# Block kernel on one core: low halves of the weights moved between GpSimd and VectorE, a fifth K tile of the modulation on TensorE, and the sines moved into the values' round

## What is computed

```python
mod = silu(c) @ w_ada + b_ada                    # 1 x 3072
shift, scale, gate = split(mod, 3)
h = rms_norm(x) * (1 + scale) + shift            # 512 x 1024
q, k, v, z_attn, xbc, dt_raw, z_ssm = split(h @ w_in)
# 16 heads of 64, for query t and key s < t:
A[t, s] = sigmoid(z_ts) * prod_{s<j<t} (1 - sigmoid(z_tj))
xbc = silu(causal_depthwise_conv(xbc, conv_w, conv_b))
```

## Time and profile before

| | us |
|---|---|
| median of 3 runs | 1807.56 (1805.79 to 1808.59) |
| the profiled execution | 1804.74 |
| its span, first to last instruction | 1803.0 |
| PE busy | 1762.1 (98%) |
| DVE, ACT, POOL busy | 907.9, 761.4, 647.8 |
| mean granted clock of PE | 0.996 of full |

### The profile page before, as it was taken

One profiled execution on the slowest core, in us unless ns is written; L12 is line 12 of the kernel. 1 busy time (PEld: TensorE's weight loads), 2 busy tenths in 40 slices (PEclk: granted clock), 3 DMA queues, 4 the chain that ended last, 5 costly groups with the idle time before them and its releaser, 6 DMA issues.

```text
span 1803.0 us, 21919 instructions
## 1 busy us (share of the span) xinstructions
PE 1762.1 (98%) x8557; PEld 1413.6 (78%) x8557; DVE 907.9 (50%) x1332; ACT 761.4 (42%) x1243; POOL 647.8 (36%) x257
## 2 busy tenths in 40 slices
PE   7999999999999999999999999999999999999998
PEld 5787777768787867867988888888866898888886
DVE  7510588874977358953543333336457253333334
ACT  3323665556345353254532222226676442223222
POOL 1343222233235233433444444444410354444442
PEclk9999999999999999999999999999999999999999
DMA  8524322221122322311232223321310222322222
GB/s 307 196 94 117 90 63 59 72 71 47 66 101 78 127 71 70 105 48 59 81 107 93 93 94 101 107 95 62 101 56 1 94 94 97 107 99 93 93 93 82
DMA packets 83921, 166.05 MB, mean 92 GB/s; under 512 B 6041, under 2 KB 8222, under 8 KB 83838
## 3 DMA queue, kind: packets, MB, share of 16 engines
q1 hardware_dynamic: 83838, 164.93, 27.9%
HBM read 157.64 MB, written 2.10 MB: 89 GB/s over the span
## 4 chain that ended last, share of the span: by engine, by line
PE 75%; issue 16%; POOL 4%; DVE 3%; ACT 1%; DMA 1%; SPq 1%; POOLq 0%; DVEq 0%; ACTq 0%
PE PDT L689 12%; PE PDT L691 12%; PE PDT L690 12%; PE PDT L700 8%; PE PDT L701 8%; PE PDT L702 8%; POOL wlo L2006 4%; PE PM L1304 2%; PE PDT L1265 2%; PE PM L1265 1%; PE PM L1231 1%; PE PDT L830 1%; PE PDT L835 1%; PE PDT L829 1%; PE PM L1163 1%
## 5 line engine op out<-in xcount | busy, mean ns | idle before, releaser
L2006 POOL TENSOR_TENSOR wlo<-wraw,whi 128x2048 fp32r<-128x2048 f32 (+5 forms) x172 | 604.9, 3527 | 1011.3 <-ACT whi L1466 1011.3
L1466 ACT ACTIVATE whi<-wraw 128x2048 fp32r<-128x2048 f32 (+2 forms) x131 | 244.0, 1862 | 518.4 <-PE PDT L691 302.1
L700 PE MATMUL PDT<-hhi,whi 128*128 128x512 f32 x796 | 312.4, 392 | 1.9 <-POOL wlo L2006 1.9
L702 PE MATMUL PDT<-hhi,wlo 128*128 128x512 f32 x796 | 310.1, 390 | 0.0
L701 PE MATMUL PDT<-hlo,whi 128*128 128x512 f32 x796 | 310.1, 390 | 0.0
L689 PE MATMUL PDT<-whi,hhi 128*128 128x512 f32 (+1 forms) x592 | 234.0, 395 | 0.4 <-POOL wlo L2006 0.4
L691 PE MATMUL PDT<-whi,hlo 128*128 128x512 f32 (+1 forms) x592 | 227.9, 385 | 0.0
L690 PE MATMUL PDT<-wlo,hhi 128*128 128x512 f32 (+1 forms) x592 | 227.8, 385 | 0.0
L689 PE MATMUL PDT<-whi,mh_hi 128*128 128x512 f32 x512 | 199.3, 389 | 0.0
L690 PE MATMUL PDT<-wlo,mh_hi 128*128 128x512 f32 x512 | 199.2, 389 | 0.0
L691 PE MATMUL PDT<-whi,mh_lo 128*128 128x512 f32 x512 | 199.2, 389 | 0.0
(11 more groups left out here) (374 smaller groups left out, 2438.2 us busy)
## 6 DMA issues: line engine op xcount, KB each, us to landing
wraw<-in_mlp_w SPq DMA_DIRECT2D x64, 1024.0 KB, 5.2
wraw<-in_w_in SPq DMA_DIRECT2D x26, 1024.0 KB, 5.2
wraw<-in_even_w_in SPq DMA_DIRECT2D x16, 1024.0 KB, 5.3
w_ada<-in_w_ada SPq DMA_DIRECT2D x11, 1024.0 KB, 13.0
wraw<-in_w_out SPq DMA_DIRECT2D x8, 1024.0 KB, 5.2
swapped<-qk_sb SPq DMA_DIRECT2D x16, 256.0 KB, 7.4
wraw<-in_even_w_out SPq DMA_DIRECT2D x4, 1024.0 KB, 4.9
wraw<-in_odd_w_o SPq DMA_DIRECT2D x4, 1024.0 KB, 5.8
```

The costliest lines, as they stand in the source:

```text
L700: mm(bank, sth, hi[:, k0 + k, :], start=start and k == 0, stop=False)
L702: last = mm(bank, stl, hi[:, k0 + k, :], start=False, stop=stop and k == 3)
L1466: nc.scalar.activation(whi[base % 2][:, 0:n], wraw[base % 2][:, 0:n], ACT.Copy).then_inc(S("w_hi"), 1)
L2006: part = g.tensor_tensor(wlo[base % 2][:, cols], wraw[base % 2][:, cols], fl(whi[base % 2][:, cols]), ALU.subtract)
```

## The change

- **Entry.** PE takes a fifth K tile of the last scale chunk (`weigh(6, 3, 1)`), and DVE takes three instead of four. PE's two folds for the second half stand in the middle of the 16 low products of `first_half(0)`, not behind them. The low half of unit 1 is made by DVE after the second modulation; POOL's first is that of unit 2, and it waits for `w_split` 2. ACT copies the last half tile of the turned x, which DVE did.
- **Values' round.** ACT's sines stand in the second round of v, with the table change behind them. PE's first scores no longer wait for the eviction of v; the first values do.
- **Heads.** POOL makes the low halves of units 16 to 21 only after the convolution with the number in a list. The low half of unit 23 is made by DVE in head 13 (`dt_head`), before its squares; that of unit 24 by POOL after the eleventh convolution, that of unit 25 after the last `sb_split`. The low half of unit 22 is now 128 columns wide on POOL, where the loop made 2048.

```diff
-        def weigh(n, bank):
+        def weigh(n, bank, more=0):
...
-                last = mm(PM[:, bank, :], silu_w[:, 4 * (n % 2) + k, :], w[:, k, :], start=k == 0, stop=k == 3)
+                last = mm(PM[:, bank, :], silu_w[:, 4 * (n % 2) + k, :], w[:, k, :], start=k == 0,
+                          stop=k == 3 and not more)
+            for k in range(more):
+                pe.wait_ge(S(f"ada_loaded{n + 1}"), 16)
+                last = mm(PM[:, bank, :], silu_w[:, 4 * ((n + 1) % 2) + k, :], wview(ADA_SLOTS[n + 1], 4, 512)[:, k, :],
+                          start=False, stop=k == more - 1)
...
-                weigh(6, 3)
+                weigh(6, 3, 1)
             unit_wait(h)
             for f in range(4):
+                if h == 0 and f == 2:
+                    fold(2, 4)
+                    fold(3, 5)
...
-                fold(2, 4)
-                fold(3, 5)
...
             if pair:
                 pe.wait_ge(S("sb_out"), pair)
+            else:
+                phase_done(pe, "v")
...
-        for name in ("q", "k", "v"):
+        for name in ("q", "k"):
             phase_done(pe, name)
...
-        rounds("v", 2, lambda i, b: vo[:, b, bass.ds(i * 512, 512)])
+        u0 = PH["v"][0]
+        for r in range(2):
+            hi(0, u0 + 2 * r + 1, 0)
+            if r:
+                act.wait_ge(S("angles"), 1)
+                nc.scalar.activation(sinall[:, :, :], ang[:, :, :], ACT.Sin).then_inc(S("sines"), 1)
+                nc.scalar.activation(ang_s[:, :, :], ang[:, :, :], ACT.Sin, scale=0.5).then_inc(S("sines"), 1)
+                nc.scalar.preload_act_table_set("natural_log_exp_and_others")
+            hi(0, u0 + 2 * r + 2, 0)
+            for b in range(4):
+                full_wait(act, "v", b, r, u0 + 2 * r + 1)
+                nc.scalar.activation(vo[:, b, 512 * r:512 * r + 512], PD[b], ACT.Copy).then_inc(S(f"bank_free{b}"), 1)
...
-        pool.wait_ge(S("w_split"), 1)
-        pairs("q", 2)
+        pool.wait_ge(S("w_split"), 2)
+        for u in range(2, 5):
+            lo(0, u, 0)
...
-        pairs("xbc", 3)
-        pairs("z_ssm", 2)
-        lo(0, PH["dt"][0] + 1, 0)
-        pairs("z_attn", 2)
+        u0 = PH["xbc"][0]
+        for n, convolved in enumerate((0, 0, 0, 2, 3, 4, 6, 7, 8, 0)):
+            if convolved:
+                pool.wait_ge(S("conv_sum"), convolved)
+            lo(0, u0 + n + 1, 0)
+        u0 = PH["z_attn"][0]
+        pool.wait_ge(S("w_split"), u0 + 1)
+        pool.wait_ge(S("conv_sum"), XBC_T - 1)
+        lo(0, u0 + 1, 0)
+        pool.wait_ge(S("sb_split"), 3 * H1)
+        lo(0, u0 + 2, 0)
+        lo(0, u0 + 3, 0)
+        lo(0, u0 + 4, 0)
...
-        weigh(7, True, (3, 3))
+        weigh(7, True, (3, 3), 1)
         modulation(1)
+        dve.wait_ge(S("w_hi"), 2)
+        v.tensor_tensor(wlo[1][:, :], wraw[1][:, :], fl(whi[1][:, :]), ALU.subtract).then_inc(S("w_split"), 1)
...
+            if h == dt_head:
+                u = PH["z_attn"][0]
+                dve.wait_ge(S("w_hi"), u + 1)
+                dve.wait_ge(S("w_split"), u)
+                v.tensor_tensor(wlo[u % 2][:, :], wraw[u % 2][:, :], fl(whi[u % 2][:, :]), ALU.subtract)\
+                    .then_inc(S("w_split"), 1)
```

More of the change, by code:

```diff
@@ L1648, in _ @@
         turned_x(TT - 1)
+        act.wait_ge(S("xt_turned"), 2 * TT)
+        nc.scalar.activation(xt[:, 4:8, (TT - 1) * P:TT * P],
+                             PD[2 * ((TT - 1) % 2) + 1].rearrange("p (k c) -> p k c", k=4), ACT.Copy)\
+            .then_inc(S("xt_read1"), 1)
         def modulated(half):
@@ L1710, in after_piece @@
                 nc.scalar.activation(dst, PD[b], ACT.Copy, scale=scale).then_inc(S(f"bank_free{b}"), 1)
-        act.wait_ge(S("angles"), 1)
-        nc.scalar.activation(sinall[:, :, :], ang[:, :, :], ACT.Sin).then_inc(S("sines"), 1)
-        nc.scalar.activation(ang_s[:, :, :], ang[:, :, :], ACT.Sin, scale=0.5).then_inc(S("sines"), 1)
         hi(0, PH["xbc"][0] + 1, 0)
-        nc.scalar.preload_act_table_set("natural_log_exp_and_others")
         for h in range(H1):
@@ L2184, in turned_x, with weigh @@
                 .then_inc(S("xt_read1"), 1)
-        def weigh(n, fresh, row=None):
+        def weigh(n, fresh, row=None, k0=0):
             dve.wait_ge(S("ada_part" if n == 3 else f"ada_loaded{n if n < 8 else n - 4}"), 16 if n < 8 else 32)
             w, a = wview(ADA_SLOTS[n if n < 8 else n - 4], 4, 512), acc[n // 2][:, :]
-            for k in range(4):
+            for k in range(k0, 4):
                 col = silu_c[:, 4 * (n % 2) + k:4 * (n % 2) + k + 1]
@@ L2193, in weigh @@
                     dve.wait_ge(S("ada_loaded3"), 16)
-                if fresh and k == 0:
+                if fresh and k == k0:
                     op = v.tensor_scalar(a, w[:, k, :], col, None, ALU.mult)
@@ L2230, in _ @@
                 turned_x(t - 1)
-        turned_x(TT - 1)
         dve.wait_ge(S("c_ready"), 1)
```

## The result

| | before | after |
|---|---|---|
| median of the runs, us | 1806.67 (1804.32 to 1808.59, 4 runs) | 1791.65 (1791.57 to 1791.81, 4 runs) |
| profiled execution, us | 1804.74 | 1791.7 |
| its span, us | 1803.0 | 1790.0 |
| mean granted clock over the span | 0.996 | 0.997 |

The ratio is 0.9918, with an interval from 0.9906 to 0.9930. The kernel gained 13.0 us between the two profiled spans, where the prediction's sum was 13.1, and 15.0 us between the medians. Of these 2.85, 0.9 is that the kernel before has 1806.67 here and had 1807.56 when the forecast was made.

The account below looks back on a forecast made before the run. The prediction took PE, busy 98% of the span, as the bound. Its terms, 5.7 (entry) + 1.7 (head 0) + 5.7 (later heads) = 13.1 us, took the median from 1807.56 to 1794.5 us, range 1791.5 to 1799.

Parts of the forecast that it names:

- The bound: Whole kernel: PE is busy 98% of the span, so time falls only by what PE stands still or runs slowly.
- The entry, 5.7: Up to unit 4: shorter DVE multiplications, folds without the long wait and full clock gain 5.7 us.
- The forecast chain: Entry: unit 1 starts at 45.0 instead of 48.75, unit 1's low products end at 55.9, unit 4 lands by 71.7.
- the margins: Entry: slack of 1.0, 0.3 and 0; the rival that one or two waits stay gave 1797.5, chance 0.14.
- the 0.3 feared at unit 2: Entry: POOL's low half of unit 2 ready at 56.2, 0.3 after PE wants it.
- two of the signs: Entry, signs of being wrong: PE waiting for `wlo` at units 1, 2 or 4; ACT waiting for unit 4's load past 71.7.
- The clock behind the folds: Entry rival: folds count as rest, unit 1 begins at clock 0.50, 2.3 us not gained, 1796.8; chance 0.10.
- Head 0, 1.7: Head 0: moving the sines brings the tails to 182.35 instead of 184.05, a gain of 1.7 us.
- The sum did not get in beside POOL: Head 0 rival: DVE's two-tile sum runs beside POOL, 1.3 us more gain, 1793.2; chance 0.07.
- Heads, 5.7: Heads 4 to 15: waits of heads 7, 11 and 15 (3.8) and head 13 (1.86) vanish, together 5.7 us.
- Theory B: Posed after the result: much of the gain, and the 2 us beyond the sum, is clock no longer falling behind PE's waits.
- Theory C: Posed after the result: parts of the change do nothing, so a few lines bring the whole gain.

Follow-up runs that it names:

- pool_unit1: Changed kernel with unit 1's low half back on POOL, fifth K tile kept: 1795.45 us, ratio 0.9939.
- the second trace: Profile of the changed kernel run once more, nothing altered: 1791.61 us, ratio 0.9911.
- four_tiles: Changed kernel with four K tiles on each side, no fifth on PE: 1791.19 us, ratio 0.9915.
- both_four_tiles: Changed kernel with unit 13's low half held until head 0's `sb_split`, unit 4's load ahead of the gate's weights, and no fifth K tile: 1789.83 us, ratio 0.9905.
- late13: Changed kernel with POOL's low half of unit 13 held until head 0's `sb_split` is complete: 1788.57 us, ratio 0.9896.
- the first experiments: Earliest follow-up runs, with the kernel before run beside them; the text does not list which ones are meant.
- entry_only: Only the entry of the change, values' round and heads as in the kernel before: 1801.82 us, ratio 0.9966.
- no_conv_wait: Changed kernel without POOL's waits for the convolutions: 1794.19 us, ratio 0.9926.
- rest_only: Only the values' round and heads of the change, entry as in the kernel before: 1797.07 us, ratio 0.9945.
- pool_unit23: Changed kernel with unit 23's low half back on POOL: 1794.65 us, ratio 0.9932.
- xt_back: Changed kernel with the copy of the last x tile back on DVE: 1790.54 us, ratio 0.9913.

## Why the prediction was right, point by point

**The bound.** Right. PE is busy 98% before and after, and the time fell by what PE stood or ran slowly.

**The entry, 5.7.** Right in its chain (pool_unit1), and right in its size when counted from unit 0. From unit 0's first product to unit 4's it is 84.11 - 26.15 = 57.96 before, 79.91 - 27.47 = 52.44 after, and 78.62 - 26.18 = 52.44 in the second trace: 5.5. The ends of these stretches before are:

```profile
26.15 1.88 PE L963 MATMUL PDT<-hhi,whi 128*128 128x512 f32 x4 [1.77 <-ACT hhi L1654]
...
84.11 0.50 PE L700 MATMUL PDT<-hhi,whi 128*128 128x512 f32 x1
```

By the clock times of the first trace only 4.2 is left, since 1.3 went at 14 to 17.5 us. The forecast chain, moved by these 1.3, holds: unit 2 at 57.2 (measured 57.13), ACT's start on unit 4 at 73.0 (72.85). Of the margins only that of unit 4 was used up. PE waited 0.55 for it, where the step had 0.1: POOL's low half took 4.93, not 4.8, and PE was there a little earlier (79.36 against 78.3 + 1.3). The 0.3 feared at unit 2 did not come: POOL is through at 57.01, and the first product that uses the low half starts at 57.62. So two of the signs that the prediction had named for being wrong came: a wait of PE for `wlo` at unit 4, and ACT's start on unit 4 past 71.7. The first is 0.55 instead of the 0.1 in the sum, and the second is the late start of 1.3; neither touches the chain.

**The clock behind the folds.** The rival fails here: with no wait, 16 folds leave the clock at 1.00. With a wait of 0.53 (four_tiles) or 0.55 (both_four_tiles) among them it fell, one trace of each; with 0.45 (late13) it stayed.

**Head 0, 1.7.** Right: from unit 4's first product to the tails 184.05 - 84.11 = 99.94 before and 98.11 after, so 1.83. The sum did not get in beside POOL: it ended at 176.44, 0.28 after POOL (176.16), the very distance of the row that the step was built on. This is as the Trainium skill has it (SBUF — State Buffer, "SBUF: two separate sides"): the engine that comes second waits for the whole of the first one's instruction. The trace agrees to within 0.14, as the sum takes 0.42 alone and ended 0.28 after POOL. late13 shows it from the other side: with POOL later the sum takes 0.43, and another 1.68 is there.

**Heads, 5.7.** The waits went as said, in heads 7, 11, 13 and 15, and nothing was late behind `conv_sum`. The term was too small. From the tails of head 0 to those of head 15 it is 398.13 - 184.05 = 214.08 before and 385.19 - 178.02 = 207.17 after: 6.9. The tails of head 15 before, with the wait that is gone:

```profile
398.13 0.45 PE L1034 MATMUL PM<-sb_hi,neg_ge 128*128 128x384 f32 x1 [1.08 <-DVE sb_lo L2353]
```

Around the single waits the traces give 1.77, 1.77, 2.15 and 1.23 for 1.37, 1.36, 1.86 and 1.08. So a wait cost about 0.15 to 0.4 more than its idle time, which the sum did not count. A part of it can be read from the traces. A product lasts 0.39, but the next one starts 0.23 behind its start; a wait is counted from the end of the last product, which leaves 0.16 out. And the first one behind a wait is followed later than usual (in head 7 by 0.28 instead of 0.18), which is another 0.1. The rest stays open.

The terms of the trace, 4.2 + 1.8 + 6.9 = 12.9, are the 13.0 of the spans: the entry's shortfall of 1.5 and the heads' surplus of 1.2 nearly cancel. That 13.0 stands so close to 13.1 is therefore in part luck. Without the 1.3 at 14 to 17.5 us the terms are 5.5 + 1.8 + 6.9 = 14.2, and the term of the sum that was too small is the heads', 5.7 for 6.9.

**From the span to the median, 0 in the prediction, 2 in fact.** This is the step that was missing. The prediction left the distance from the profiled execution to the median as it was; it is 1.9 before (1806.67 against 1804.74) and none after (1791.65 against 1791.7). In before's 9 executions beside the first experiments the mean clock is 0.994 to 0.997 and the time 1804.52 to 1809.05, the fastest with 0.997. A mean clock that is 0.003 lower over 1803 us costs 5.4 us (an estimate: PE is busy nearly all the time), enough for all of this scatter. The profiled execution of before (0.996, 1804.74) was one of the better ones. The changed kernel has 0.997 to 0.998 and 1790.15 to 1791.87. So two waits of before had a second price, a fall of the clock behind them in some executions: 1.57 behind head 0's, 1.55 behind that of unit 23. Behind the waits of 1.36 in heads 7 and 11 no fall is in the traces that have them (before, entry_only, no_conv_wait). Theory B thus holds beside A for the scatter, and is the likely cause of the 2 us. That before's slower executions lose their time at these waits is argued from entry_only, rest_only and pool_unit23 and not shown, since none of them was profiled itself.

**Theory C.** Unit 1's move (3.8), unit 23's (3.0), the wait for the convolutions (2.5) and the sines' (1.8) each carry a part. The fifth tile's is not to be told by itself, and the copy's move to ACT brings nothing that can be told (xt_back's median is 1.1 lower, but the kernel before was 0.9 lower beside it too, and the ratios are 0.9913 and 0.9911).

## What to carry to other kernels

On a kernel whose PE is busy 98%, list PE's waits and price each three times: its idle time, some tenths of a us for starting again, and the chance that the clock falls behind it (here 1.3 to 1.6 us, in three of eight traces behind a wait of 1.5). Judge a change of a few waits by the medians and the spread of many executions, since one profiled execution can lie 2 us from the median by the clock alone. A GpSimd instruction of several us belongs behind the two-SBUF-input work of VectorE that PE waits for, and holding it there (late13) was worth as much as moving the sines.

## What was not expected of the hardware

- The clock falls to its lower level behind a wait of 1.51 in one execution of the changed kernel and not in another. Behind waits of 1.5 to 2.1 us in head 0 and at unit 23 it fell in some traces and not in others, and in two it fell behind 0.53 and 0.55 with short folds around them. Such a fall costs 1.3 to 1.6 us.
- At 14 to 17 us the lower level came in 3 of 11 traces that have the copy of x on ACT and in none of 3 that have it on DVE. The fall begins before the copy's place, and so few traces do not show that the copy has a part in it. It stays open.
- DVE makes a low half (128x2048) in 2.29 us where POOL takes 4.6, and up to 5.12 with DVE's work in between.
